# A new block order for the first projections, layer norm's steps at piece borders of the last blocks, and the convolution's sample columns on GpSimd

## What is computed

```python
z = h @ w_in                       # columns: q, k, v (512 each), then pre_glu (2 x 512)
a, g = jnp.split(pre_glu, 2, axis=-1)
u = a * jax.nn.sigmoid(g)
u_ext = jnp.concatenate([conv_hist, u], axis=1)
y = depthwise_conv(u_ext, conv_w, width=31) + conv_b
y = jax.nn.silu(layernorm(y, ln_g, ln_b))      # norm over the 512 channels
att = band_attention(q, k, v, rel_bias)
out = jnp.concatenate([att, y], axis=-1) @ w_out
```

## Time and profile before

| | |
|---|---|
| median of 3 runs | 3093.26 us (3092.72 to 3100.05) |
| profiled execution, its own time | 3096.99 us |
| its span | 3095.3 us |
| PE busy | 2911.2 us (94%) |
| DVE busy | 1439.9 us (47%) |
| ACT busy | 701.3 us (23%) |
| POOL busy | 143.0 us (5%) |
| mean granted clock of PE | 0.97 |

### The profile page before, as it was taken

How to read it: one execution, slowest core, us unless ns; L and a number is a source line. 1 busy time by engine, 2 the same in 40 slices (tenths; PEclk the granted TensorE clock), 3 DMA queues, 4 the chain that set the end, 5 groups by cost and what they waited for, 6 DMA issues and landing times.

```text
span 3095.3 us, 50807 instructions
## 1 busy us (share of the span) xinstructions
PE 2911.2 (94%) x21228; PEld 2802.1 (91%) x21228; DVE 1439.9 (47%) x2479; ACT 701.3 (23%) x1148; POOL 143.0 (5%) x235
## 2 busy tenths in 40 slices
PE   5999699979999999999799999989799999999996
PEld 5998367969999999999799999989699999999996
DVE  6888576252333333333634445454623333333335
ACT  3111465031111111111322222231221111111111
POOL 4000211010000000000100000000100000000001
PEclk9999699989999999999899999999899999999998
DMA  3111331101111111111111111112111111111111
GB/s 124 42 48 68 95 131 76 48 21 55 42 42 41 42 41 42 41 43 46 75 49 43 43 43 51 57 54 79 36 55 42 41 42 49 47 41 42 41 35 62
DMA packets 51269, 163.50 MB, mean 53 GB/s; under 512 B 8480, under 2 KB 19664, under 8 KB 48512
## 3 DMA queue, kind: packets, MB, share of 16 engines
q1 hardware_dynamic: 46624, 148.98, 13.9%
q10 hardware_dynamic: 3456, 8.91, 0.8%
q0 software_dynamic: 992, 2.62, 0.4%
HBM read 143.15 MB, written 18.92 MB: 52 GB/s over the span
## 4 chain that ended last, share of the span: by engine, by line
PE 87%; DVE 7%; issue 2%; ACT 2%; DMA 1%; POOL 1%; ACTq 0%; DVEq 0%; POOLq 0%; SPq 0%
PE PS L574 19%; PE PS L576 19%; PE PS L575 19%; PE PS L814 6%; PE PS L815 6%; PE PS L816 6%; DVE HF L685 2%; PE PS L1214 1%; PE PS L1483 1%; PE PS L1221 1%; PE PS L1599 1%; PE PS L1600 1%; PE PS L1601 1%; PE PS L1245 1%; DVE HBL L695 1%
## 5 line engine op out<-in xcount | busy, mean ns | idle before, releaser
L574 PE MATMUL PS<-HAH,WH 128*128 128x384 f32 x1776 | 615.5, 347 | 11.3 <-DVE HBL L695 7.4
L575 PE MATMUL PS<-HAL,WH 128*128 128x384 f32 x1776 | 601.0, 338 | 0.0
L576 PE MATMUL PS<-HAH,WL 128*128 128x384 f32 x1776 | 600.3, 338 | 0.0
L576 PE MATMUL PS<-HBH,WL 128*128 128x384 f32 x1776 | 594.5, 335 | 0.0
L574 PE MATMUL PS<-HBH,WH 128*128 128x384 f32 x1776 | 594.3, 335 | 0.0
L575 PE MATMUL PS<-HBL,WH 128*128 128x384 f32 x1776 | 594.3, 335 | 0.0
L562 DVE TENSOR_TENSOR WL<-WR,WH 128x1024 fp32r<-128x1024 f32 x201 | 244.2, 1224 | 566.5 <-ACT WH L557 564.9
L814 PE MATMUL PS<-UH,WH 128*128 128x384 f32 x1056 | 357.4, 338 | 5.2 <-issue 5.0
L574 PEld LDWEIGHTS PS<-HAH,WH 128*128 128x128 f32 x1776 | 338.5, 191 | 24.0 <-issue 12.2
L815 PE MATMUL PS<-UL,WH 128*128 128x384 f32 x1056 | 356.4, 338 | 0.0
L816 PE MATMUL PS<-UH,WL 128*128 128x384 f32 x1056 | 356.3, 337 | 0.0
(11 more groups left out here) (234 smaller groups left out, 2636.1 us busy)
## 6 DMA issues: line engine op xcount, KB each, us to landing
WR<-w_fi_in SPq DMA_DIRECT2D x88, 512.0 KB, 3.5
WR<-w_fo_in SPq DMA_DIRECT2D x44, 512.0 KB, 3.4
WR<-w_c_in SPq DMA_DIRECT2D x32, 512.0 KB, 4.0
WR<-w_ab_in SPq DMA_DIRECT2D x20, 512.0 KB, 3.5
CACHES<-k_cache_in SPq DMA_DIRECT2D x8, 1024.0 KB, 4.8
CACHES<-v_cache_in SPq DMA_DIRECT2D x8, 1024.0 KB, 6.9
X<-x_t_in SPq DMA_DIRECT2D x3, 1536.0 KB, 10.7
x_spill<-X SPq DMA_DIRECT2D x1, 4608.0 KB, 12.3
```

The lines of the kernel that those rows point to most:

```text
L574: nc.tensor.matmul(out, wh, hh(k, third(n)), start=(k == 0), stop=False)
L575: nc.tensor.matmul(out, wh, hl(k, third(n)), start=False, stop=False)
L576: mm = nc.tensor.matmul(out, wl, hh(k, third(n)), start=False, stop=(k == KT - 1))
```

## The change

The 20 blocks get a fixed order (`AB_ORDER`): g and a come early, the four k blocks last. Blocks are numbered from 0 here. The steps of the layer norm on PE stand ahead of pieces of blocks 17, 18 and 19 (`LN_AT`), and ACT's and DVE's steps with them. The taps of the samples leave DVE and go to POOL as two instructions each: a `tensor_scalar` (tap times weight into a scratch tile `TAPS`) and a `tensor_tensor` (add to `Y`). On DVE the prompt's taps follow each other directly, and each waits for the one before. The low parts of the weights have new places between the taps (`LOWER`). POOL loads the bias tables ahead of its taps, and sends the two outputs ahead of the taps of the last group. The tables `BT` and `BS` are shifted before the layer norm instead of after it. The tile of squares `LSQ` now lies over `EV` and `UP` and no longer over `US`, so that ACT's wait for the outputs is gone; DVE has it ahead of the attention. In the attention the first two chunks come ahead of the first stream. The streams' caches are loaded once the last k block is done.

```diff
+        ORDER = []
+        for c in range(NCK):
+            ORDER += [(c, f, None) for f in range(PAIRS)]
+            if 1 <= c <= NB:
+                ORDER.append((None, None, c - 1))
...
+        AB_ORDER = [(k, int(j)) for k, j in "g0 a0 v0 g1 a1 q0 v1 g2 a2 q1 v2 g3 a3 q2 v3 q3 k0 k1 k2 k3".split()]
...
@@ pool_program
-            pool.wait_ge(s_cv, 2 * CW * AB)
-            pool.wait_ge(s_co, AB)
-            pool.dma_start(cvp_o, CO[:, :, :]).then_inc(s_outc, 16)
-            pool.dma_start(cvs_o, US[:, :, :, NS:HIST + NS]).then_inc(s_outc, 16)
-            pool.wait_ge(s_outc, 32)
-            pool.wait_ge(s_full["vt"], N3 * AB)
...
+            for j in range(AB):
+                pool.wait_ge(s_got["a"], N3 * (j + 1))
+                if j == AB - 1:
+                    pool.wait_ge(s_co, AB)
+                    pool.dma_start(cvp_o, CO[:, :, :]).then_inc(s_outc, 16)
+                    pool.dma_start(cvs_o, US[:, :, :, NS:HIST + NS]).then_inc(s_outc, 16)
...
+                def scaled(t):
+                    frames, w = US[:, j, :, t:t + NS], sm("cw", j * CW + t)
+                    if t > 2:
+                        pool.wait_ge(s_ct, j * (CW - 1) + t - 2)
+                    if t == 0:
+                        ins = pool.tensor_scalar(out, frames, w, sm("cb", j), ALU.mult, ALU.add)
+                    else:
+                        ins = pool.tensor_scalar(tap(t), frames, w, None, ALU.mult)
+                    ins.then_inc(s_cs, 1)
...
+                scaled(0)
+                scaled(1)
+                for t in range(1, CW):
+                    if t + 1 < CW:
+                        scaled(t + 1)
+                    pool.wait_ge(s_cs, j * CW + t + 1)
+                    need(pool, s_ct, j * (CW - 1) + t - 1)
+                    pool.tensor_tensor(out, out, tap(t), ALU.add).then_inc(s_ct, 1)
+            pool.wait_ge(s_ct, AB * (CW - 1))
...
@@ ab_pe
+            LN_AT = {(17, 1): sums, (17, 2): squared, (18, 0): spread, (18, 1): squared, (18, 2): spread,
+                     (19, 0): squared, (19, 1): spread}
...
+                for n in range(N3):
+                    if (i, n) in LN_AT:
+                        LN_AT[(i, n)](pe, T)
...
+        def sums(pe, T):
+            pe.wait_ge(s_got["q"], N3 * AB)
+            pe.wait_ge(s_cv, CW * AB)
+            pe.wait_ge(s_ct, (CW - 1) * AB)
+            for n in range(N3):
+                for j in range(AB):
+                    mm = nc.tensor.matmul(PS[:, n, 0:TH], ones[:, :], Y[:, j, third(n)], start=(j == 0), stop=(j == AB - 1))
+                mm.then_inc(s_ms, 1)
...
@@ ab_dve
+            LOWER = {(0, 2): 4, (0, 10): 5, (0, 19): 6, (1, 1): 7, (1, 4): 8, (1, 12): 9, (1, 21): 10,
+                     (2, 1): 11, (2, 5): 12, (2, 14): 13, (2, 23): 14, (3, 1): 15, (3, 8): 16, (3, 17): 17, (3, 26): 18}
+
+            def conv(j):
+                for t in range(CW):
+                    if (j, t) in LOWER:
+                        cut_lo(dve, T, LOWER[(j, t)] % 3)
+                    src, out, w = UP[:, t:t + SEQ], Y[:, j, 0:SEQ], sm("cw", j * CW + t)
+                    if t == 0:
+                        ins = dve.tensor_scalar(out, src, w, sm("cb", j), ALU.mult, ALU.add)
+                    else:
+                        dve.wait_ge(s_cv, j * CW + t)
+                        ins = dve.scalar_tensor_tensor(out=out, in0=src, scalar=w, in1=out, op0=ALU.mult, op1=ALU.add)
+                    ins.then_inc(s_cv, 1)
...
@@ ln_act
-            act.wait_ge(s_outc, 32)
```

More of the change, by code:

```diff
@@ L946, in ffn_dve @@
                 dve.tensor_tensor(xs, xs, out, ALU.add).then_inc(s_x, 1)
[L949 to L976, removed]
@@ new lines, in squared, with spread @@
+        def squared(pe, T):
+            if T("ln") == 0:
+                pe.wait_ge(s_got["vt"], N3 * AB)
+            n = T("ln")
+            T.add("ps", 1)
+            pe.wait_ge(s_ps, T("ps"))
+            for tt in range(TPT):
+                mm = nc.tensor.matmul(PS[:, 7, 3 * n + tt:3 * n + tt + 1], LSQ[:, 0, tile(tt)], ones[:, 0:1],
+                                      start=True, stop=True)
+            mm.then_inc(s_ms, 1)
+        def spread(pe, T):
+            n = T("ln")
+            T.add("dg")
+            pe.wait_ge(s_dg, T("dg"))
+            nc.tensor.matmul(PS[:, cast_bank(n), 0:TH], ones[:, :], LDG[:, :, :].rearrange("p a b -> p (a b)"),
+                             start=True, stop=True).then_inc(s_rb, 1)
+            T.add("ln")
@@ L978, in ab_act, with token_major @@
         def ab_act(act, T):
-            def token_major(j, n, three):
-                need(act, s_full["vt"], three + n + 1)
-                act.activation(VTOK[:, 3 * n:3 * n + 3, bass.ds(j * P, P)],
+            def token_major(j, n):
+                act.wait_ge(s_full["vt"], N3 * j + n + 1)
+                act.activation(VTOK[:, 3 * n:3 * n + 3, j * P:(j + 1) * P],
                                PS[:, 6 + n % 2, 0:TH].rearrange("p (a b) -> p a b", b=P), ACT.Copy).then_inc(s_got["vt"], 1)
[L984 to L989, removed]
-                for n in range(N3):
[L991 to L996, removed]
-                for n in range(N3):
[L998 to L1028, removed]
-                        w = sm("cw", j * CW + t)
-                        if t == 0:
-                            ins = dve.tensor_scalar(out, src, w, sm("cb", j), ALU.mult, ALU.add)
-                        else:
-                            need(dve, s_cv, T("cv") - 1)
-                            ins = dve.scalar_tensor_tensor(out=out, in0=src, scalar=w, in1=out, op0=ALU.mult, op1=ALU.add)
-                        ins.then_inc(s_cv, 1)
-                        T.add("cv")
-            def step(j, first=False):
-                three = T("j3")
-                cut_lo(dve, T, 1)
-                if not first:
-                    conv(j - 1, 28, CW)
-                cut_lo(dve, T, 2)
-                need(dve, s_co, T("co"))
-                need(dve, s_cv, T("cv"))
-                for n in range(N3):
-                    need(dve, s_full["a"], three + n + 1)
-                    need(dve, s_got["g"], three + n + 1)
@@ new lines, in square, with root @@
+        def square(act, T):
+            n = T("lsq")
+            act.wait_ge(s_yc, n + 1)
+            if n:
+                act.wait_ge(s_ms, T_MS + N3 + n)
+            act.activation(LSQ[:, :, :], Y[:, :, third(n)], ACT.Square).then_inc(s_sq, 1)
+            T.add("lsq")
+        def root(act, T):
+            n = T("lrt")
+            act.wait_ge(s_ms, T_MS + N3 + n + 1)
+            act.activation(rt[:, 3 * n:3 * n + 3], PS[:, 7, 3 * n:3 * n + 3], ACT.Sqrt,
+                           bias=eps[:, 0:1], scale=1.0 / AW).then_inc(s_rt, 1)
+            T.add("lrt")
@@ L1343, in att_dve @@
         def att_dve(dve, T):
[L1345 to L1347 removed]
+            dve.wait_ge(s_outc, 32)
             dve.memset(PRE[:, :, CACHE + CHK:5 * P], 0.0).then_inc(s_bias, 1)
```

238 lines of the change are left out of this document (136 added, 102 removed).

## The result

| | before | after |
|---|---|---|
| median | 3092.99 us (4 runs) | 3126.73 us (4 runs, 3124.7 to 3131.77) |
| profiled span | 3095.3 us | 3124.1 us |
| first exponential of the attention | 349.35 us | 385.06 us |

The changed kernel takes 1.011 of the time before (95% interval 1.0087 to 1.0133): 33.7 us more by the medians, 28.8 by the spans. The first exponential comes 35.7 us later than in the earlier trace rows. From there to the first matmul of the output projection the new kernel needs 175.1 us instead of 181.0, and behind it the two are equal (2564.0 and 2564.9 us).

The account below looks back on a forecast made before the run. The bound was PE's gap between projections and attention, a serial layer norm chain. S at 316, plus 56.2 and 3 for the clock, put the first exponential at 375.2, 26 us later: 3119 us, range 3084 to 3144.

Parts of the forecast that it names:

- Rival D: At SBUF, taps and POOL do not exclude each other; 27.5 us faster, 3066 us; chance 0.17.
- rival B: Each POOL instruction costs DVE its whole duration, 0.35 us on average; DVE ends at 304, 52 us slower; chance 0.10.
- rival C: About even: holds cost DVE nothing, or two POOL instructions per gap, each 4 us slower; both, 10 us faster; chance 0.13.
- S: The time at which PE really starts the layer norm's sums over channels, forecast at 316 us.
- DVE's taps end with no turns: DVE's convolution taps, low parts and gates, undisturbed by POOL, summed from 69.3 us to an end at 255.4.
- rest on POOL: POOL's sample instructions left when DVE's taps are through: 90 at 0.40 us, 36 us.
- S to the first exponential: From PE's sums to the attention's first exponential on ACT: 56.2 us, plus 3 for PE's low clock.
- I take 0.10, nearer to the short cast: DVE's loss beside a POOL `tensor_scalar`: 0.10 us; with the add's 0.22, 0.16 on average for a turn.
- The nearest row is the select over 128 columns with 0.292 us: Price taken for POOL's `tensor_scalar` in the samples' taps; POOL's instructions then 0.35 us on average, 0.40 with a wait.
- some 5 more in each of the three gates: POOL's extra instructions during DVE's gates, beside the 139 in turns; about 154 of 244 done when DVE's taps end.
- A step that came 1 us late at all six borders: Layer norm steps between PE's projection pieces: such lateness would cost 6 us, but was costed at nothing.
- The clock: PE's clock is low at first after its idle wait for the sums: 3 us added, an estimate.

Follow-up runs that it names:

- e1: The changed kernel with the samples' taps of all four groups back on DVE; median 3077.45 us, ratio 0.9936 to the kernel before.
- e2: The changed kernel with only the first tap of each group's samples on POOL, the other 30 left out; 3065.87 us, ratio 0.9899.
- e5: The changed kernel with 240 of POOL's 244 instructions made memsets that only write, leaving out those samples' taps; 3069.44 us, ratio 0.9921.
- e10: e1's kernel, with POOL also doing the changed kernel's 244 instructions into a tile that nobody reads; 3112.43 us, ratio 1.0054.
- e4: The changed kernel with the attention's items in the order of before; 3126.88 us, ratio 1.0097.
- e7: e1's kernel with the layer norm's steps on PE two pieces later; 3068.41 us, ratio 0.9918.
- e8: e1's kernel with the layer norm's steps behind all the projections, as before the change; 3071.47 us, ratio 0.9931.

## Why the prediction came out right

**The mechanism** is the one forecast: POOL's reads and DVE's two-input taps take turns, and PE waits for POOL with eight pieces of projections behind it. e1 (POOL's taps away), e2 (away and not replaced) and e5 (as many instructions, no reads) end the 60.95 us wait for POOL: PE does not wait in e2 and e5, and in e1 it waits 11.51 us, for DVE. Rival D (no exclusion) falls by the rows of POOL at 1.20 and 1.46 us, and rival B (whole holds) by DVE's end at 264.4 instead of 304. Of rival C, the half in which POOL gets two instructions into a gap falls by the 141 done; the other half, a hold that costs DVE nothing, is nearly what was measured (0.06 us a turn), but it put S at 294 with POOL's pace of 0.40. The Trainium skill ("SBUF — State Buffer", section "Who interferes with whom") says that only GpSimd's reads meet a DVE instruction with two SBUF inputs, not its writes; the memsets of 206 ns agree. The exclusive lock for the whole instruction that the same page gives (section "SBUF: two separate sides") agrees with POOL's durations, but not with DVE's loss: 0.06 us for a POOL instruction that takes 0.45 or 0.60 us alone.

**The sizes**, term by term:

| term | predicted | measured |
|---|---|---|
| PE ready for the sums, nothing late | 265.6 | 266.0 (e2), 263.4 (e5), 265.1 (the changed kernel) |
| DVE's taps end with no turns | 255.4 | 256.8 (e5) |
| cost of a turn to DVE | 0.16 | 0.06 |
| DVE's taps end | 277.6 | 264.4 |
| POOL's instructions done by then | 154 | 141 |
| rest on POOL | 90 x 0.40 | 103 x 0.57 |
| output DMAs' issue | 2.3 | 2.4 |
| S | 316 | 326.0 |
| S to the first exponential | 59.2 | 59.0 |
| first exponential, against before | +26 | +35.7 |

Three terms were mis-sized, not all in the same direction. "I take 0.10, nearer to the short cast", 0.16 with the add, was three times too much, because I took the cost from DVE instructions that follow each other with nothing between them. Here each tap waits for the one before, and I read the rest as part of POOL's turn falling into that wait: a turn costs 0.05 between two prompt taps, but 0.15 behind a low part, which waits for no tap, and 0.13 in e10, where sample taps fill the wait. This put DVE's end 13 us too late. "The nearest row is the select over 128 columns with 0.292 us" was half of what the `tensor_scalar` takes alone, 0.60, and the average of 0.57 in place of 0.40 adds 15 us to my 90 instructions. The third term is the gates: they left 103 instructions and not 90, another 7 us, so the rest on POOL is 59 us where I had 36. Together S is 10 us later than forecast, and so is the first exponential, by 9.9. That the error of DVE's end took back more than half of the other two is luck.

The term of the gates was too large: "some 5 more in each of the three gates" makes 154, and POOL did 141. At each gate 3 of its instructions ended, 9 in all. The other 132 fell to DVE's 139, since beside six low parts and the very first tap none of POOL's ended. That a gate gives 3 and not 5 fits POOL's pace: a gate lasts about 2 us, and POOL's instructions take 0.45 and 0.60 us even alone.

That DVE's end without turns came out so near (255.4 and 256.8) is luck too. I let the first tap start at 69.3, where it started before. In e5 it starts at 74.2, in the changed kernel at 73.3, behind a low part that now stands ahead of the gate (70.53). The taps and gates together took 182.6 us in e5 and not 186.1.

**The costs put at nothing.** "A step that came 1 us late at all six borders" showed at one border only: PE waits 1.54 us for the diagonal ahead of the last spread, in the changed kernel as in e2 and e5. **The clock:** from S to the first exponential it is 57.5 us in e2 and in e5, where PE does not stand still ahead of the sums, and 59.0 in the changed kernel, where the granted clock is 0.63 from 326 to 330 us. The sums take 9.4 us there and 7.9 in e2, so the low clock cost 1.5 us and not 3. Without it the stretch is 1.3 us longer than my 56.2, about as much as the late step. The two misses cancel, and that 59.2 came out right is luck. The attention's order, 0 within 3 us, measured -5.9 in the profile of the changed kernel but nothing in the medians of e4. **The gain** that I named as hidden by POOL was 27.5 us; e2 has 25.9 of it at the first exponential and 31 by its ratio, but it leaves work out. With the samples where they were, on DVE, the first exponential comes 14 us earlier than before (e1), and with the layer norm's steps a little later 25 (e7), because DVE with the samples is through at 275.5, 10 us behind PE.

## What to carry to other kernels

Before work moves from a busy engine to an idle one, count instructions, not busy time: beside a dense stream of two-input DVE instructions, POOL gets one reading instruction for each, so 244 of them need 244 of DVE's, and DVE had 139. What a shared resource costs each side must be priced apart: here the turns cost the engine that was relieved 8.5 us, and the idle one took 252 us for work of about 130. And a wait placed in the middle of an engine's program holds up everything behind it; put it where its data surely is there (e7), or at the end if that isn't known (e8).

## What the runs showed that I had not expected

- The pace of POOL beside DVE does not depend on its size: 1.25 and 1.34 us for 16 columns, 1.20 and 1.46 us for 128.
- A turn costs DVE next to nothing at 16 columns, 0.05 us at 128 when each DVE instruction waits for the one before, and 0.13 to 0.15 us when DVE has other work in that wait.
- A short sample tap of DVE's (0.35 us) mostly lets POOL wait on: 150 turns for some 260 instructions (e10).
- POOL's `tensor_scalar` on 128 columns in 8 rows of 16 takes 0.60 us alone, a `tensor_tensor` 0.45 and a `memset` 0.21; at 16 columns 0.33 and 0.22. The 112 columns between them cost 0.27 and 0.23 us, so by an estimate nearly half of the time at 128 is not for the columns.
